# State-space rounds: where the decay masks are made, and the order of XTE, XDT and a weight remainder

## What is computed

```python
def step(state, inp):
    xc, bc, cc, dtc, dac = inp
    cum = jnp.cumsum(dac, axis=1)
    seg = cum[:, :, None] - cum[:, None, :]
    decay = jnp.exp(jnp.where(mask, seg, -jnp.inf))
    cb = jnp.einsum('btgn,bsgn->btsg', cc, bc)
    xdt = xc * dtc[..., None]
    y = jnp.einsum('btsg,btsgr,bsgrp->btgrp', cb, decay, xdt)
    y = y + jnp.einsum('btgn,bgrpn->btgrp', cc, state) * jnp.exp(cum)[..., None]
    to_end = jnp.exp(cum[:, -1:] - cum)
    state = jnp.exp(cum[:, -1])[..., None, None] * state \
        + jnp.einsum('bsgn,bsgrp->bgrpn', bc, xdt * to_end[..., None])
    return state, y
```

## Time and profile before

| | |
|---|---|
| median of 3 runs | 1857.17 us (1856.9 to 1858.33) |
| profiled execution, its own time | 1856.05 us |
| its span, first to last instruction | 1854.3 us |
| TensorE busy | 1812.5 us, 98% |
| VectorE busy | 971.9 us, 52% |
| ScalarE busy | 609.6 us, 33% |
| GpSimd busy | 156.4 us, 8% |
| mean granted clock of TensorE | 0.993 |

### The profile page before, as it was taken

One profiled execution on the slowest core, in us unless ns is written; L12 is line 12 of the kernel. 1 busy time (PEld: TensorE's weight loads), 2 busy tenths in 40 slices (PEclk: granted clock), 3 DMA queues, 4 the chain that ended last, 5 costly groups with the idle time before them and its releaser, 6 DMA issues.

```text
span 1854.3 us, 26241 instructions
## 1 busy us (share of the span) xinstructions
PE 1812.5 (98%) x9852; PEld 1509.9 (81%) x9852; DVE 971.9 (52%) x1360; ACT 609.6 (33%) x942; POOL 156.4 (8%) x138
## 2 busy tenths in 40 slices
PE   7999999989999999999999999999999999999997
PEld 5888888867888888788888888887888888888885
DVE  6444443367888888742434444555433644444333
ACT  4323222233343333342223334443322422222221
POOL 4111100023111111100000000000000011111000
PEclk9999999999999999999999999999999999999998
DMA  4322223322222222122322222223222322323331
GB/s 154 102 95 97 98 94 110 105 68 69 68 68 75 72 68 74 63 91 92 101 69 69 92 90 75 84 80 100 93 100 93 95 98 91 102 90 102 102 104 66
DMA packets 47353, 164.92 MB, mean 89 GB/s; under 512 B 5520, under 2 KB 6672, under 8 KB 47296
## 3 DMA queue, kind: packets, MB, share of 16 engines
q1 hardware_dynamic: 43584, 158.10, 26.1%
q10 hardware_dynamic: 3712, 6.03, 1.1%
HBM read 162.01 MB, written 2.10 MB: 89 GB/s over the span
## 4 chain that ended last, share of the span: by engine, by line
PE 70%; issue 21%; DVE 5%; POOL 2%; ACT 1%; DMA 0%; DVEq 0%; POOLq 0%; ACTq 0%; SPq 0%
PE G L547 33%; PE G L598 12%; PE I L547 9%; PE G L563 7%; DVE WL L1462 2%; PE I L915 1%; POOL hid L442 1%; PE I L949 1%; PE I L925 1%; PE I L726 1%; DVE CV L1626 1%; PE I L734 1%; PE G L783 1%; DVE UL L1478 1%; ACT SH L1171 0%
## 5 line engine op out<-in xcount | busy, mean ns | idle before, releaser
L1462 DVE TENSOR_TENSOR WL<-RAW,WH 128x1024 fp32r<-128x1024 f32 x297 | 387.6, 1308 | 298.7 <-ACT WH L1044 290.3
L1044 ACT CAST WH<-RAW 128x1024 fp32r<-128x1024 f32 x297 | 308.8, 1045 | 230.5 <-PE I L547 126.4
L547 PE MATMUL G<-UH,WH 128*128 128x512 f32 x1136 | 284.0, 392 | 0.0
L547 PE MATMUL G<-UL,WH 128*128 128x512 f32 x1136 | 280.6, 389 | 0.0
L547 PE MATMUL G<-UH,WL 128*128 128x512 f32 x1136 | 280.6, 389 | 0.0
L547 PEld LDWEIGHTS G<-UH,WH 128*128 128x128 f32 x1136 | 211.5, 188 | 47.5 <-issue 4.4
L547 PEld LDWEIGHTS G<-UL,WH 128*128 128x128 f32 x1136 | 213.2, 188 | 44.4
L547 PEld LDWEIGHTS G<-UH,WL 128*128 128x128 f32 x1136 | 213.2, 188 | 44.3
L598 PE MATMUL G<-WH,UH 128*128 128x256 f32 x640 | 91.9, 287 | 4.1 <-DVE WL L1462 4.1
L598 PE MATMUL G<-WL,UH 128*128 128x256 f32 x640 | 90.8, 285 | 0.0
L442 POOL TENSOR_TENSOR hid<-hid,rms 128x512 f32<-128x512 f32 x44 | 57.1, 1298 | 397.9 <-ACT hid L1078 397.9
(11 more groups left out here) (291 smaller groups left out, 2153.0 us busy)
## 6 DMA issues: line engine op xcount, KB each, us to landing
RAW<-in_slabs SPq DMA_DIRECT2D x297, 512.0 KB, 3.3
h<-in_x SPq DMA_DIRECT2D x4, 512.0 KB, 6.9
bias<-in_rel ACTq DMA_DIRECT2D x16, 128.0 KB, 2.9
out_y<-h ACTq DMA_DIRECT2D x8, 256.0 KB, 2.2
bias<-in_rel ACTq DMA_DIRECT2D x16, 112.0 KB, 2.8
cst<-in_cst SPq DMA_DIRECT2D x1, 168.0 KB, 3.8
ut<-in_wgk SPq DMA_DIRECT2D x3, 32.0 KB, 8.7
```

The lines of the kernel that those rows point to most:

```text
L547: ins = mm(dst, W[:, n.slot, (k - k0) * P:(k - k0 + 1) * P], R[:, k, :], start=begin and which == 0 and k == k0, stop=end and which == 2 a ...
L1044: nc.scalar.copy(WH[:, n.slot, :], RAW[:, n.slot, :]).then_inc(split_hi, 1)
L1462: V.tensor_tensor(WL[:, n.slot, :], RAW[:, n.slot, :], WH[:, n.slot, :].bitcast(F32), ALU.subtract).then_inc(split_lo, 1)
```

## The change

- MSL and MSH are made from SC, the table of all heads, with the group's four columns taken by an address computed from the round number, and no longer from the copy gsc. The masks' form is now tile, head, frame, one dimension more.
- `da_lo(g + 1)` is issued by GpSimd in round g, behind XD and ahead of rstd. It waits for the intra products of group g. The first one runs ahead of the loop.
- MSH becomes a function of its own, `da_hi`, issued behind the last SiLU step of the round and ahead of `ssm_scale`; it waits for the decay sums of the group before.
- In `ssm_x` XTE is made first and XDT second; GpSimd's XD now waits for XDT. In the loop's t = 0, `ssm_x` comes ahead of the weight remainder.

```diff
             def da_lo(g):
 
-                pool.wait_ge(sems["group_const"], after("group_const", g))
                 pool.wait_ge(sems["intra_done"], last("intra_done", g - 1))
-                inc(nc.gpsimd.tensor_tensor(MSL[:].rearrange("p (q t) -> p q t", t=CH),
-                                            bc(gsc[:, 28:32, :].rearrange("p j r -> p (j r)"), CH),
-                                            causal[:].unsqueeze(1).to_broadcast([P, TT * HPG, CH]), ALU.mult),
+                inc(nc.gpsimd.tensor_tensor(MSL[:].rearrange("p (j r t) -> p j r t", j=TT, t=CH),
+                                            bc(SC[:, 28:32, bass.ds(HPG * g, HPG)], CH), causal_all, ALU.mult),
                     "da_lo_masked")
 
-            def ssm(g):
-
-                pool.wait_ge(sems["xte_ready"], after("xte_ready", g))
+            def ssm(g, ahead=True):
+
+                pool.wait_ge(sems["xdt_ready"], after("xdt_ready", g))
                 pool.wait_ge(sems["group_norm"], after("group_norm", g))
                 d = ggrp[:, 2:6].unsqueeze(1).unsqueeze(3).to_broadcast([P, TT, HPG, CH])
                 x4 = XD[:].rearrange("p j (r c) -> p j r c", r=HPG)
                 inc(nc.gpsimd.tensor_tensor(x4, x4, d, ALU.mult), "xd_ready")
+                if ahead:
+                    da_lo(g + 1)
                 pool.wait_ge(sems["ssm_var"], after("ssm_var", g))
...
-            with pool.Fori(0, NG) as i:
-                da_lo(i)
+            da_lo(0)
+            with pool.Fori(0, NG - 1) as i:
                 ssm(i)
+            ssm(NG - 1, False)
...
                 inc(V.tensor_copy(gsc[:], SC[:, :, bass.ds(HPG * g, HPG)]), "group_const")
                 dve.wait_ge(sems["group_const"], after("group_const", g))
-                dve.wait_ge(sems["intra_done"], last("intra_done", g - 1))
-                da = gsc[:, 24:28, :].rearrange("p j r -> p (j r)")
-                inc(V.tensor_tensor(MSH[:].rearrange("p (q t) -> p q t", t=CH), bc(da, CH),
-                                    causal[:].unsqueeze(1).to_broadcast([P, TT * HPG, CH]), ALU.mult), "da_hi_masked")
+
+            def da_hi(g):
+
+                dve.wait_ge(sems["seg_done"], after("seg_done", g - 1))
+                inc(V.tensor_tensor(MSH[:].rearrange("p (j r t) -> p j r t", j=TT, t=CH),
+                                    bc(SC[:, 24:28, bass.ds(HPG * g, HPG)], CH), causal_all, ALU.mult), "da_hi_masked")
...
             def ssm_x(g):
                 dve.wait_ge(sems["x_copied"], after("x_copied", g))
                 dve.wait_ge(sems["intra_done"], last("intra_done", g - 1))
+                inc(V.tensor_tensor(XTE[:]..., ALU.mult), "xte_ready")
                 inc(V.tensor_tensor(XDT[:]..., ALU.mult), "xdt_ready")
-                inc(V.tensor_tensor(XTE[:]..., ALU.mult), "xte_ready")
...
                 dve.wait_ge(dt_pool, DA_SPLIT)
+                da_hi(0)
                 group_scalars(0)
...
                     conv_taps(p, t, n + t, wn + t)
-                    lo(n + t + 3)
                     if t == 0:
                         ssm_x(inner)
+                    lo(n + t + 3)
...
                     if t == 3:
                         ssm_y(inner)
                     conv_silu(p, t)
+                da_hi(p)
                 ssm_scale(inner)
```

More of the change, by code:

```diff
@@ L339, in bc @@
             return ap.unsqueeze(len(ap.shape)).to_broadcast(list(ap.shape) + [n])
+        causal_all = causal[:].unsqueeze(1).unsqueeze(1).to_broadcast([P, TT, HPG, CH])
         def over_tiles(ap):
@@ L1664, in ssm_x @@
                 dve.wait_ge(sems["intra_done"], last("intra_done", g - 1))
+                inc(V.tensor_tensor(XTE[:].rearrange("p j (r c) -> p (j r) c", c=CH), heads(XD[:].rearrange("p j c -> p (j c)")), rows(2),
+                                    ALU.mult), "xte_ready")
                 inc(V.tensor_tensor(XDT[:].rearrange("p j (r c) -> p (j r) c", c=CH), heads(XD[:].rearrange("p j c -> p (j c)")), rows(1),
                                     ALU.mult), "xdt_ready")
-                inc(V.tensor_tensor(XTE[:].rearrange("p j (r c) -> p (j r) c", c=CH), heads(XD[:].rearrange("p j c -> p (j c)")), rows(2),
-                                    ALU.mult), "xte_ready")
             def ssm_m(g):
```

## The result

The changed kernel takes 1860.22 us against 1857.01 for the kernel before (medians of 20 runs each): ratio 1.0018, 95% interval 1.0012 to 1.0025. That is 3.2 us slower. The interval excludes no change: all of it lies between 0.12% and 0.25% slower. The profiled execution took 1860.05 us, its span is 1858.3 us; the one before took 1856.05 us, so the two profiles are 4.0 us apart where the medians are 3.2 apart.

The account below looks back on a forecast made before the run. TensorE, busy 98% of the span, bounds the kernel through its waits. New Y waits 10.0, less 6.8 in the loop and 0.9 in the last group, give +2.3 us: median 1859.5 us, range 1850.2 to 1863.0.

Parts of the forecast that it names:

- case A: Last group: clock falls to 1.2 GHz in the new 2.8 us wait, losing 1.6 us; 1861.1 us, chance 0.2.
- The ceiling: TensorE's waits for XTE and MSL: at most some 7 to 8 us of 1856 to gain; 6.8 in rounds 1 to 6.
- the template: Round 0 of the kernel before, 43.93 us with neither wait, on which the new order was replayed.
- Part 1: MSL moved from the round's tail to behind XD: starts 467.71, ends 469.62; gains its share of 1.13 us a round.
- B: GpSimd released later than taken, still ahead of the remainder; each 0.1 us costs 0.7; 1862.0 us, chance 0.15.
- C: Remainder goes ahead of MSL, which then holds nobody; wait for Y 0.13 us; 1850.4 us, chance 0.15.
- Part 2: XTE ahead of XDT and remainder: XTE over 2 us early; XD holds SiLU, next taps 0.41 us later.
- Part 3: MSL holds the remainder before the Y steps: new 1.43 us wait for Y in rounds 0 to 6, 10.0 us.
- Part 4: MSH behind the round's last SiLU: 1.23 us inside VectorE's 1.74 us wait for the squares, cost nothing.
- Case D: Idle time for MSH isn't there: 0.7 us a round, 4.9 us on top; 1864.4 us, chance 0.03.
- Part 5: Last group: XTE 2 us earlier, state chain only 0.9 us earlier; TensorE waits some 2.8 us; gain 0.9.
- The condition for the exclusion: VectorE instructions with two SBUF inputs and GpSimd ones reading SBUF exclude each other for a whole instruction.

Follow-up runs that it names:

- the order of XTE alone: Kernel before with only XTE, XDT, then weight remainder reordered and XD released by XDT; masks at old places: ratio 1.0020 to the kernel before.
- the masks alone: Changed kernel with the old order of XDT, XTE and remainder, XD released by XTE; masks at new places: ratio 1.0014 to the kernel before.

## Why the prediction was right, and where it wasn't

**The median**: 1859.5 was forecast, 1860.22 measured, inside the likeliest case's own range. The forecast was +2.3 us and +3.2 came. The median lies 0.7 us above the forecast and 0.9 below case A's 1861.1, so by itself it doesn't tell one from the other; the profiles do.

**The ceiling and the template** held. The two waits cost 314.25 - 307.51 = 6.7 us in the loop (6.8 forecast), and kernels without any wait in the loop land on 7 x 43.93 us to 0.03.

**Part 1**: MSL's start was taken as 467.71 and came at 467.73; its duration of 1.91 us was right, though table, address and dimensions are new. The release by TensorE, which no row had shown, takes about 0.2 us (the intra products end at 467.52). B and C are out: MSL was neither late nor behind the remainder.

**Part 2**: SiLU 2.40 us (forecast 2.4), the next taps at 450.64 (450.62). XD was held by the remainder as forecast.

**Part 3**: remainder 2.52 us (2.5), first Y step at 470.64 (470.62), transposes of Y at 480.48 (480.48). The new wait is (317.45 - 307.51) / 7 = 1.42 us a round (1.43). Moving the remainder takes it away, moving MSL takes away all but 0.14 us, and taking out XD's hold doesn't.

**Part 4**: no cost, 0.61 us left in the gap (0.5). Case D is out.

**Part 5**: the chain did come 0.9 us earlier: from the transposes of x to the inter products 14.81 us, against 771.43 - 755.74 = 15.69. The wait for SS was 2.88 us (2.8).

**The step that failed is the choice between the forecast and case A.** I held the clock to stay up behind a single gap and gave A 0.2. In or behind a wait of 2.88 us it fell in five profiles of six, and never in the four in which no wait of the last group was over 1.75 us. A's price was 1.6 us; from the table the last group is longer than 32.13 - 0.88 = 31.25 by 1.65 us in the changed kernel, and by 1.4 to 2.7 us in the other four. With it the sum for the profiled execution is 1856.05 + 2.3 + 1.6 = 1860.0, and 1860.05 was measured. That the median came within 0.7 us of the forecast all the same is in part luck: the profiled execution of the kernel before was 1 us below its median, that of the changed kernel 0.2 below. The changed kernel's 20 runs spread from 1857.9 to 1863.2, the kernel before's from 1855.5 to 1858.6. The mean granted clock of the changed kernel was 0.994 in its two fastest runs and 0.991 in its four slowest, though 0.994 also stands beside one of 1860.12. That fits, loosely, a clock that falls in some executions and lasts longer in some, but only profiled runs show where it falls.

**The condition for the exclusion** was too narrow: I had it as two SBUF inputs. It didn't touch the forecast, since no such scaling stood beside MSL, but it misled me about the next place for MSL, where a gain of 5.0 us was expected and the kernel came out slower.

## What to carry to other kernels

Idle time of GpSimd is no free place: ask which of VectorE's instructions stand beside it, and put a GpSimd instruction beside those that read PSUM. A work moved off the path can be given back with interest by what it holds, here 1.42 us a round for the 1.13 that were won; and the cure can be the order of two instructions on the other engine. Where several waits stand in a round, replay one round without a wait by its rows: that gave the starts in round 0 of the changed kernel that were forecast to 0.03 us. It needs care where one round leads into another, as the order of XTE alone showed (+3.0 us for the +1.3 expected).

## What the runs showed of the hardware

- A plain scaling from SBUF to SBUF (tensor_scalar, 128 x 256 float32, one tensor) is shut out by a GpSimd instruction just as one with two SBUF tensors is: four took 2.77 us beside MSL, 1.14 alone. The same size with a PSUM operand took 1.65 us beside MSL and 1.66 alone. I had not expected the first. The Trainium skill has it in the page "SBUF — State Buffer", section "Who interferes with whom": tensor_scalar can run in a mode that uses both ports, and contends then. The trace fits that: a quarter of the four is 0.29 us, against 0.41 with the PSUM operand; that it is this mode was not shown otherwise.
- Who is held when both start within 0.2 us: MSL 0.05 us ahead of a remainder held it for 1.7 us, and at 0.07 us ahead it held the scalings. In the earlier trace rows GpSimd won from 0.04 us behind, the only row of that kind. In the earlier trace rows it lost from 0.12 us behind, and in the changed kernel from 0.16 us behind (XD at 447.34 took 2.83 us, remainder at 447.18).
- TensorE's granted clock fell from 2.4 to 1.2 GHz in or just behind a wait of 2.88 us in the midst of solid work, in five profiles of six, and in the kernel before in the wait of 2.33 us for XTE (0.50 in windows of 1 us from 762 to 765). It stayed up in the two profiles with waits of 1.45 and 1.75 us and 7.7 us of work between them. A wait cut in two may cost less than one piece: with the masks alone the last group took 31.26 us, in the changed kernel 32.90.
